# First block's attentions: one group of attention products a step, then the dense products

## Chip, cores and metric
One NeuronCore of a Trainium2 chip runs the whole program. The metric is the device time of one execution in microseconds (us), smaller is better; the kernel before takes 2327.96 (median of 3 runs, 2321.61 to 2328.72).

## What is computed
Two transformer blocks on 256 tokens (and, in the first block, 256 context tokens) of width 1024, all in float32. The first block has two layers. Each layer: a gated feed-forward net, three attentions that share one input projection and one output projection, and a second feed-forward net. The second block (a recurrent mix, latent attention, differential attention, a convolutional feed-forward net) is not touched by the change. The attentions of a layer, cut to what matters:

```python
p = u @ w_in[l]                       # q, k, v of all heads
y_w = _window_attn(q_w, k_w, v_w, ck_w, cv_w, sink_win[l])      # 6 heads, window and sink
y_g = _global_attn(q_g, k_g, v_g, ck_g, cv_g)                   # 4 heads, q and k normed
y_n = _neighbourhood_attn(q_n, k_n, v_n, ck_n, cv_n, rpb_nbr[l])  # 6 heads, bias
h = h + gm * (concatenate([y_w, y_g, y_n]) @ w_out[l])
if not last:                          # layer 0 alone: the context attends to itself
    hc = hc + cgm * (yc @ w_out[l])
```

Each attention is softmax(q k^T / 8 + mask or bias) v over the 256 tokens and the 256 context tokens.

## The kernel before
**Dense products.** Activations lie with features on the partitions and tokens along the free dimension. A float32 product is done as three with rounded halves: `three` (L1212) issues high x high (L1214), high x low (L1215) and low x high (L1216) for one k-step of 128 rows. The weights come from memory in panels of 1024 KB into two buffers (`raw`); ScalarE makes the high half of a panel (`whi`), VectorE the low one (`wlo`). In the stretches of the change this is done in four pieces, `split_piece` (L588): pieces 0 and 2 on ScalarE (L598, L600), 1 and 3 on VectorE (L608).

**Order.** Every engine executes its own instructions strictly in the order in which the program issues them. The engines meet by semaphores only. So the order of the Python calls is the schedule: a call that issues to ScalarE queues there behind all that earlier calls put there.

**The stretch of the change** is a layer's attention stage (`for l in range(L1)`, about L1590 to L2066). Two things are interleaved there by hand.

One is the generator `program` (L1875): the input projection in 18 tiles (`in_tile`, L1663; the order of q, k and v tiles is `IN_TILES`, L61) and the output projection in 16 (`out_tile`, L1818), with small jobs in between or inside a tile: `turn` (L1789) multiplies a q or k chunk by a permutation, for the rotary embedding, whose three VectorE operations are L1800, L1801 and L1803; `v_turn` (L1726) transposes a value tile from `v_feat`. A tile or job takes one of two accumulator banks (6 and 7) by `next_bank` (L1633), which makes TensorE wait until what was last in that bank is copied out. A job inside a tile takes the other bank than that tile, the one that the next tile will take. The copying out (`evacuate`, L1718 for q, L1720 for k, L1712 for v, L1738 for the turned values) is issued at the next `flush` (L1871), in the second k-step of the following tile or near its end. The generator yields a cost in us (0.69 for a k-step of 512 columns, 0.36 for 256); `fill(us)` (L1906) takes from it until the costs are used up. `need` (L1916) takes from it until an input is prepared, and its costs are taken off the following fills.

The other is the attention itself, one unit at a time: a unit is two heads (a chunk c of 128 features), a stream (0 the tokens, 1 the context, in layer 0 alone) and a half of 128 queries. Layer 0 has 32 units, four to a chunk (stream 0 twice, then stream 1 twice; "a quad"); layer 1 has 16, all of stream 0. For a unit:

- `scores` (S, product L1936): queries by keys, 512 keys for stream 0, 256 for stream 1, into a pair of banks (0 and 1 or 2 and 3). It waits for the exponentials of the unit two before.
- `exponentials` (exp): on VectorE mask or bias (L1959), maximum (L1960), for windowed heads the sink (L1964, L1966), for global ones the norm (L1970); on ScalarE two exponentials (L1974) and for windowed heads one more of the sink (L1978).
- `normalise` (norm): VectorE, reciprocal (L1987, with L1986 for the sink) and two scalings of the probabilities (L1990).
- `transposes(i, s)` (T0 and T1, product L2004): four transposes of the probabilities of head s into bank 4, which ScalarE copies out (`probs_t`, L2011). Both begin with a wait of TensorE for norm and for the last copy out of bank 4. For a context unit T1 does both heads, and T0 does nothing but that wait.
- `values` (V, L2026), at each odd unit: 16 products for stream 0, 8 for stream 1, into bank 5.
- `split_y` (y), at each odd unit: y_hi on ScalarE (L2037), y_lo on VectorE (L2039).

Step i of the loop at L2045 issues, before the change, in this order: T0(i-2), S(i+1), exp(i), norm(i-1), a fill of half the step's share, T1(i-2), V(i-3), y(i-4), a fill of the other half. A step's share is 4 us of costs in stream 0 and 2 in stream 1. `share` and what a fill takes in all are as before in the changed kernel.

Of the kernel before, what the change touches and what calls it, by code (L numbers as in the profile page):

```python
# [748 lines left out]
def build(nc, ins, out):  # L749
# [48 lines left out]
    def cst(name, width=P, k=0):  # L798
        o = CC.at[name] + k
        if o >= CC.kept:  # L800
            return tables[0][:, o - tables[1]:o - tables[1] + width]
        return const[:, o:o + width]

    def vcol(name, k=0, width=1):
        o = VC.at[name] + k
        if o >= VC.kept:
            return vec_2[:, o - VC.kept:o - VC.kept + width]
        return vec[:, o:o + width]
# [294 lines left out]
    def root_table(function=ACT.Sqrt):  # L1103

        act.do(act.q.activation(root_warm[:, :], cst("eps", 1), function))
# [451 lines left out]
    for l in range(L1):  # L1557
# [348 lines left out]
        def fill(us):  # L1906

            ahead[0] += us
            while ahead[0] > 0 and not all_heads_left[0]:
                cost = next(work)  # L1910
                if cost is None:
                    all_heads_left[0] = True
                else:
                    ahead[0] -= cost

        def need(*keys):  # L1916

            while any(k not in prepared for k in keys):
                ahead[0] -= next(work)

        units = [(c, stream, qt) for c in ATT for stream in range(streams_q) for qt in range(2)]
# [3 lines left out]
        def kind_of(i):  # L1925
            return head_at(units[i][0], 0)[0]

        def scores(i):
            c, stream, qt = units[i]
            kc = head_at(c, 0)[2]  # L1930
            need(("q", c), ("k", kc))
            o, key0 = stream * S + qt * P, stream * S
            pe.after(prepared["q", c], prepared["k", kc], (st.s_ev, st.groups), marks[i - 2]["exp"] if i >= 2 else None)
            for s in range(2):
                rows_ = slice(64 * s, 64 * s + 64)
                r = pe.q.matmul(banks[2 * (i % 2) + s][:, 0:T - key0], qT[rows_, c, o:o + P], kT[rows_, kc, key0:T],  # L1936
                                start=True, stop=True)
            marks[i]["scores"] = pe.do(r)

        def exponentials(i):  # L1940
            c, stream, qt = units[i]
            kind = kind_of(i)
            nk = T - stream * S
            b = bank_pairs[i % 2][:, :].rearrange("p (s n) -> p s n", s=2)
            k, m = i % 3, marks[i]
            dve.after(m["scores"])
            bias = None
            if stream == 0 and kind == "win":
                bias, left = cst("win_mask", S, qt * S).rearrange("p (o n) -> p o n", o=1).to_broadcast([P, 2, S]), b[:, :, 0:S]
                dve.after(tab_ready)  # L1950
            if stream == 0 and kind == "nbr":
                need(("nbr", c))
                dve.after(prepared["nbr", c])
                first = NBR_DR - NBR_ROWS - 2 * qt
                h0_ = 2 * (c - 5)
                bias = nbr[:, h0_:h0_ + 2, first:first + NBR_ROWS, :].rearrange("p h r c -> p h (r c)")
                left = b[:, :, 0:S]
            if bias is not None:
                dve.after(dve.do(dve.q.tensor_tensor(left, left, bias, ALU.add)))  # L1959
            mx = dve.do(dve.q.tensor_reduce(out=stat[:, k, 0, :], in_=b[:, :, 0:nk], axis=AX.X, op=ALU.max, negate=True))  # L1960
            scale = [1.0, 1.0]
            if kind == "win":
                dve.after(mx, sink_ready)
                mx = dve.do(dve.q.tensor_tensor(stat[:, k, 0, :], stat[:, k, 0, :], neg_sink[:, 2 * c:2 * c + 2], ALU.min))  # L1964
                dve.after(mx)
                over = dve.do(dve.q.tensor_tensor(stat[:, k, 2, :], stat[:, k, 0, :], vcol(("sink", l), 2 * c, 2), ALU.add))  # L1966
            if kind == "glob":
                o = 8 * (c - 3) + 2 * (2 * stream + qt)
                dve.after(mx, prepared["rms"])
                mx = dve.do(dve.q.tensor_tensor(stat[:, k, 0, :], stat[:, k, 0, :], rms[:, o:o + 2], ALU.mult))  # L1970
                scale = [rms[:, o + s:o + s + 1] for s in range(2)]
            act.after(mx, marks[i - 3]["transposed"] if i >= 3 else None)
            for s in range(2):
                m["exp"] = act.do(act.q.activation(pbuf[k][:, s, 0:nk], b[:, s, 0:nk], ACT.Exp, bias=stat[:, k, 0, s:s + 1],  # L1974
                                                   scale=scale[s], accum_out=stat[:, k, 1, s:s + 1]))
            if kind == "win":
                act.after(over)
                m["sink"] = act.do(act.q.activation(stat[:, k, 2, :], stat[:, k, 2, :], ACT.Exp))  # L1978

        def normalise(i):  # L1980
            c, stream, qt = units[i]
            nk = T - stream * S
            k, m = i % 3, marks[i]
            dve.after(m["exp"], m.get("sink"))
            if "sink" in m:
                dve.after(dve.do(dve.q.tensor_tensor(stat[:, k, 1, :], stat[:, k, 1, :], stat[:, k, 2, :], ALU.add)))  # L1986
            dve.after(dve.do(dve.q.reciprocal(stat[:, k, 3, :], stat[:, k, 1, :])))  # L1987
            for s in range(2):
                pb = pbuf[k][:, s, 0:nk]
                m["norm"] = dve.do(dve.q.tensor_scalar(pb, pb, stat[:, k, 3, s:s + 1], None, ALU.mult))  # L1990
# [3 lines left out]
        def transposes(i, s):  # L1994
            c, stream, qt = units[i]
            nt = 4 - 2 * stream
            k, m, quad = i % 3, marks[i], i // 2
            pe.after(m["norm"], copied[0])
            if stream and s == 0:
                return  # L2000
            heads_ = range(2) if stream else [s]
            for x, hd in enumerate(heads_):
                for t in range(nt):
                    r = pe.q.transpose(banks[4][:, (x * nt + t) * P:(x * nt + t + 1) * P], pbuf[k][:, hd, t * P:(t + 1) * P],  # L2004
                                       cst("ident"))
            m["transposed"] = pe.do(r)
            act.after(m["transposed"], quads_done.get(quad - 2))
            dst = ptb[quad % 2][:, s, :, qt * P:(qt + 1) * P] if not stream else ptb[quad % 2][:, :, 0:nt, qt * P:(qt + 1) * P]
            src = banks[4][:, :].rearrange("p (t q) -> p t q", q=P) if not stream else \
                banks[4][:, :].rearrange("p (s t q) -> p s t q", s=2, q=P)  # L2010
            copied[0] = act.do(act.q.activation(dst, src, ACT.Copy))  # L2011
            m["copied"] = copied[0]

        def values(i):

            if i % 2 == 0:
                return
            c, stream, _ = units[i]
            nt, quad = 4 - 2 * stream, i // 2
            kc = head_at(c, 0)[2]  # L2020
            need(("v", kc))
            pe.after(prepared["v", kc], marks[i]["copied"], quads_done.get(quad - 1))
            for t in range(nt):
                for s in range(2):
                    vo = head_at(c, s)[3]
                    r = pe.q.matmul(banks[5][64 * s:64 * s + 64, 0:S], vt[:, t + 2 * stream, vo:vo + HD],  # L2026
                                    ptb[quad % 2][:, s, t, :], start=(t == 0), stop=(t == nt - 1))
            marks[i]["pv"] = pe.do(r)
# [16 lines left out]
        for i in range(len(units) + 4):  # L2045
            here = min(i, len(units) - 1)
            share = 1.33 if units[here][1] == 0 else 0.67
            if 2 <= i < len(units) + 2:
                transposes(i - 2, 0)
            if i + 1 < len(units):  # L2050
                scores(i + 1)
            if i < len(units):
                exponentials(i)
            if 1 <= i <= len(units):
                normalise(i - 1)
            fill(1.5 * share)
            if 2 <= i < len(units) + 2:
                transposes(i - 2, 1)
            if 3 <= i < len(units) + 3:
                values(i - 3)  # L2060
            if i >= 4:
                split_y(i - 4)
            fill(1.5 * share)
            if i == len(units):
                root_table()
        for _ in work:  # L2066
# [1125 lines left out]
```

## Time and profile before

| | us |
|---|---|
| median of 3 runs | 2327.96 (2321.61 to 2328.72) |
| profiled execution | 2326.03 |
| its span in the trace | 2324.7 |
| TensorE busy | 2260.5 (97%) |
| VectorE busy | 1490.9 (64%) |
| ScalarE busy | 964.4 (41%) |
| attention stage of layer 0, in the span | about 430 to 640 |
| attention stage of layer 1 | about 1400 to 1550 |

How to read it: the span runs from the first to the last recorded instruction of one execution. PE is TensorE's products, PEld its weight loads, DVE is VectorE, ACT is ScalarE, POOL is GpSimd. TensorE's products are pipelined, so the time of one is best read from the start of one to the start of the next, and "busy" is no measure of how well it is used. A float32 product with full precision appears as more than one record. In a wait, the engine and line behind the arrow are what released it. PEclk is the clock that TensorE was granted, as a share of 2.4 GHz.

### The profile page before, as it was taken

How to read it: one execution, taken by the hardware profiler on the slowest of the kernel's cores; microseconds unless marked ns; L12 is line 12 of the kernel's file. 1: busy time of each engine (PE TensorE's matmuls, PEld its weight loads, DVE VectorE, ACT ScalarE, POOL GpSimd, SP SyncE). 2: the span in 40 equal slices, each digit the busy share in tenths (PEclk: the TensorE clock that was granted, in tenths of full speed). 3: DMA queues.
4: the chain of work that ended last, by engine and by line, in shares of the span. 5: the costliest groups of instructions: out<-in, count | busy, mean ns of one | idle time of the engine just before them, and what ended most of it. 6: DMA issues, size and time to landing. Idle time of an engine off the chain costs nothing. (4 is left out here: it accounts for less than half of the span.)

```text
span 2324.7 us, 37251 instructions
## 1 busy us (share of the span) xinstructions
PE 2260.5 (97%) x14432; PEld 1920.7 (83%) x14432; DVE 1490.9 (64%) x2302; ACT 964.4 (41%) x1555; POOL 393.9 (17%) x381
## 2 busy tenths in 40 slices
PE   9999999999999999999999999989999999999998
PEld 6888887666778888888888876679998998898998
DVE  5756766465676666676564345666667766777874
ACT  5222224455442222242222244554446335656763
POOL 1000001100010000000000011049996575000000
PEclk9999999999999999999999999999999999999999
DMA  7654543311234444434443323124554332244544
GB/s 297 221 187 162 180 162 129 106 37 55 73 118 181 171 173 161 170 139 163 162 180 130 100 103 108 58 89 178 178 175 157 110 103 91 77 157 159 189 165 143
DMA packets 53911, 331.05 MB, mean 142 GB/s; under 512 B 6688, under 2 KB 7968, under 8 KB 23328
## 3 DMA queue, kind: packets, MB, share of 16 engines
q1 hardware_dynamic: 50336, 319.15, 38.6%
q0 software_dynamic: 3456, 10.25, 1.6%
q8 instruction: 83, 1.36, 0.2%
q14 instruction: 36, 0.29, 0.0%
HBM read 325.56 MB, written 3.80 MB: 142 GB/s over the span
## 5 line engine op out<-in xcount | busy, mean ns | idle before, releaser
L1214 PE MATMUL bank<-u_hi,whi 128*128 128x512 f32 (+1 forms) x2352 | 805.2, 342 | 4.8 <-ACT qT L1716 1.6
L1215 PE MATMUL bank<-u_lo,whi 128*128 128x512 f32 (+1 forms) x2352 | 789.7, 336 | 0.0
L1216 PE MATMUL bank<-u_hi,wlo 128*128 128x512 f32 (+1 forms) x2352 | 789.6, 336 | 0.0
L585 DVE TENSOR_TENSOR wlo<-raw,whi 128x2048 fp32r<-128x2048 f32 (+2 forms) x203 | 423.6, 2086 | 307.5 <-ACT whi L581 297.8
L1214 PEld LDWEIGHTS bank<-u_hi,whi 128*128 128x128 f32 x2352 | 443.1, 188 | 82.3 <-issue 27.8
L581 ACT ACTIVATE whi<-raw 128x2048 fp32r<-128x2048 f32 (+2 forms) x203 | 345.5, 1702 | 346.3 <-PE bank L1216 296.0
L1216 PEld LDWEIGHTS bank<-u_hi,wlo 128*128 128x128 f32 x2352 | 443.3, 188 | 47.5
L1215 PEld LDWEIGHTS bank<-u_lo,whi 128*128 128x128 f32 x2352 | 442.9, 188 | 44.6 <-issue 0.2
L1289 ACT ACTIVATE sil<-bank 128x512 f32<-128x512 f32 (+1 forms) x88 | 48.0, 545 | 519.4 <-PE bank L1216 516.6
L1214 PE MATMUL bank<-hidden_hi,whi 128*128 128x512 f32 x528 | 205.4, 389 | 0.0
L1215 PE MATMUL bank<-hidden_lo,whi 128*128 128x512 f32 x528 | 205.4, 389 | 0.0
L1216 PE MATMUL bank<-hidden_hi,wlo 128*128 128x512 f32 x528 | 205.4, 389 | 0.0
L643 POOL TENSOR_TENSOR wlo<-raw,whi 128x512 fp32r<-128x512 f32 x16 | 21.4, 1335 | 971.6 <-ACT whi L627 971.5
L943 DVE SCALAR_TENSOR_TENSOR bank<-raw,c_row 128x1024 f32<-128x1024 f32 x128 | 157.2, 1228 | 8.5 <-DMA raw<-in_stream 7.4
L1407 POOL TENSOR_TENSOR rel_bias_map<-rel_bias_map,bucket_step 128x384 f32<-128x384 f32 x124 | 158.1, 1275 | 10.4
L943 DVE SCALAR_TENSOR_TENSOR raw<-raw,bank 128x1024 f32<-128x1024 f32 x128 | 155.7, 1217 | 0.0
L1293 DVE TENSOR_TENSOR prod<-sil,bank 128x512 f32<-128x512 f32 (+1 forms) x88 | 54.6, 621 | 157.3 <-ACT sil L1289 154.3
L608 DVE TENSOR_TENSOR wlo<-raw,whi 128x1024 fp32r<-128x1024 f32 (+2 forms) x84 | 99.3, 1193 | 73.3 <-ACT whi L598 69.7
L1404 POOL TENSOR_SCALAR bucket_step<-in_bucket,bucket_steps 128x384 f32<-128x384 f32 x124 | 131.5, 1060 | 12.4
L1216 PEld LDWEIGHTS bank<-hidden_hi,wlo 128*128 128x128 f32 x528 | 99.1, 188 | 20.7
L1215 PEld LDWEIGHTS bank<-hidden_lo,whi 128*128 128x128 f32 x528 | 99.1, 188 | 20.6
L1214 PEld LDWEIGHTS bank<-hidden_hi,whi 128*128 128x128 f32 x528 | 99.1, 188 | 20.4
(450 smaller groups left out, 3204.9 us busy)
## 6 DMA issues: line engine op xcount, KB each, us to landing
raw<-in_stream SPq DMA_DIRECT2D x229, 1024.0 KB, 4.8
raw<-in_stream SPq DMA_DIRECT2D x80, 704.0 KB, 4.0
first_ada<-in_stream SPq DMA_DIRECT2D x8, 1024.0 KB, 16.7
raw<-in_stream SPq DMA_DIRECT2D x8, 768.0 KB, 4.2
skew<-rpb_rows POOLq DMA_DIRECT2D x8, 336.0 KB, 6.3
nbr_bias<-skew POOLq DMA_DIRECT2D x24, 112.0 KB, 5.9
h<-in_tokens SPq DMA_DIRECT2D x4, 512.0 KB, 5.6
raw<-in_stream SPq DMA_DIRECT2D x8, 256.0 KB, 16.8
```

Of the source, the lines that this page charges most:

```text
L581: a.activation(self.hi[to][:, 0:n], raw[:, 0:n], ACT.Copy).then_inc(self.s_hi, 1)
L585: v.tensor_tensor(self.lo[to][:, 0:n], raw[:, 0:n], self.hi[to][:, 0:n].bitcast(F32), ALU.subtract).then_inc(self.s_lo, 1)
L608: r = v.q.tensor_tensor(self.lo[to][:, cols], self.raw[slot][:, cols], self.hi[to][:, cols].bitcast(F32), ALU.subtract)
L643: r = v.q.tensor_tensor(self.lo[to][:, cols], self.raw[slot][:, cols], self.hi[to][:, cols].bitcast(F32), ALU.subtract)
L943: r = dve.q.scalar_tensor_tensor(out=product, in0=w, scalar=1.0, in1=rows, op0=ALU.mult, op1=ALU.mult, accum_out=to)
L1214: pe.q.matmul(dst, w[0], x[0], start=start, stop=False)
L1215: pe.q.matmul(dst, w[0], x[1], start=False, stop=False)
L1216: return pe.q.matmul(dst, w[1], x[0], start=False, stop=stop)
L1289: act.q.activation(sil[par][:, 0:n], banks[2 * par][:, 0:n], ACT.Silu).then_inc(s_sil, 1)
L1293: dve.q.tensor_tensor(prod[par][:, 0:n], sil[par][:, 0:n], banks[2 * par + 1][:, 0:n], ALU.mult).then_inc(st.s_ev, 1)
L1404: z = pool.do(pool.q.tensor_scalar(step[:, :], bucket[:, :], 1.0 - start, steps[:, hh, b + 1:b + 2], ALU.add, ALU.mult))
L1407: z = pool.do(pool.q.tensor_tensor(rel[:, hh, :], rel[:, hh, :], step[:, :], ALU.add))
```

## The change
In each step the second half's transposes T1 of unit i-2, the scores, the values and y now stand together at the step's start; norm(i-1) is issued ahead of them, exp(i) behind them; T0, now of unit i-1, closes the group; then comes one fill with the costs of both. Everything else is the same.

```diff
@@ -2045,22 +2045,21 @@
         for i in range(len(units) + 4):
             here = min(i, len(units) - 1)
             share = 1.33 if units[here][1] == 0 else 0.67
+            if 1 <= i <= len(units):
+                normalise(i - 1)
             if 2 <= i < len(units) + 2:
-                transposes(i - 2, 0)
+                transposes(i - 2, 1)
             if i + 1 < len(units):
                 scores(i + 1)
-            if i < len(units):
-                exponentials(i)
-            if 1 <= i <= len(units):
-                normalise(i - 1)
-            fill(1.5 * share)
-            if 2 <= i < len(units) + 2:
-                transposes(i - 2, 1)
             if 3 <= i < len(units) + 3:
                 values(i - 3)
             if i >= 4:
                 split_y(i - 4)
-            fill(1.5 * share)
+            if i < len(units):
+                exponentials(i)
+            if 1 <= i < len(units) + 1:
+                transposes(i - 1, 0)
+            fill(3 * share)
             if i == len(units):
                 root_table()
         for _ in work:
```

Step i in the changed kernel: norm(i-1), T1(i-2), S(i+1), V(i-3), y(i-4), exp(i), T0(i-1), fill.

## Rows read from the trace of the kernel before

**Rows 1.** The page's first line: the span.
```profile
span 2324.7 us, 37251 instructions
```

**Rows 2.** Windows: length; busy PE, PEld, DVE, ACT, POOL; PEclk, DMA share, GB/s.
```profile
430.00:640.00 210.00, 202.82 (x1056) 140.96 (x1056) 128.21 (x284) 108.37 (x253) 0.00 (x0) 1.00 0.15 55
1400.00:1550.00 150.00, 140.87 (x855) 105.36 (x855) 91.05 (x171) 77.03 (x159) 8.01 (x12) 1.00 0.24 78
```

**Rows 3.** Waits of TensorE, 430 to 640: us in total, times, longest.
```profile
PE bank L1936 <- ACT probs_t L2011: 1.6, 2, 0.8
...
PE bank L1795 <- ACT qT L1718: 0.9, 2, 0.7
...
PE bank L1936 <- DVE probs L1990: 0.8, 1, 0.8
```

**Rows 4.** Waits of TensorE, 1400 to 1560.
```profile
PE bank L1732 <- ACT inv_norm_diagonal L1712: 3.3, 2, 1.9
PE bank L2004 <- ACT probs_t L2011: 2.0, 2, 1.2
```

**Rows 5.** Timeline, TensorE, steps 7 and 8 of layer 0: start, duration, instruction, [idle before].
```profile
474.92 0.60 PE L2004 MATMUL bank<-const,probs 128*128 128x128 f32 x4
476.30 1.13 PE L1936 MATMUL bank<-kT,qT 64*128 64x512 f32 x4 [0.78 <-ACT probs_t L2011]
```

**Rows 6.** Timeline, TensorE, block edges in layer 0.
```profile
485.59 0.70 PE L1936 MATMUL bank<-kT,qT 64*128 64x256 f32 x4
486.22 0.50 PE L1214 MATMUL bank<-u_hi,whi 128*128 128x512 f32 x1
486.56 0.39 PE L1215 MATMUL bank<-u_lo,whi 128*128 128x512 f32 x1
486.79 0.39 PE L1216 MATMUL bank<-u_hi,wlo 128*128 128x512 f32 x1
...
487.72 0.60 PE L2004 MATMUL bank<-const,probs 128*128 128x128 f32 x4
488.07 0.48 PE L1214 MATMUL bank<-u_hi,whi 128*128 128x512 f32 x1
```

**Rows 7.** Timeline of three engines, steps 11 and 12 of layer 0.
```profile
499.19 0.60 ACT L2011 ACTIVATE probs_t<-bank 128x512 f32<-128x512 f32 x1 [1.48 <-PE bank L2004]
...
499.68 0.38 ACT L2037 ACTIVATE y_hi<-bank 128x256 fp32r<-128x256 f32 x1
...
500.09 0.42 DVE L2039 TENSOR_TENSOR y_lo_k<-bank,y_hi 128x256 fp32r<-128x256 f32 x1 [2.94 <-ACT y_hi L2037]
...
502.61 0.69 ACT L1974 ACTIVATE probs<-bank,stat 128x512 f32<-128x512 f32 x1 [2.06 <-DVE stat L1964]
...
503.47 0.60 PE L2004 MATMUL bank<-const,probs 128*128 128x128 f32 x4
503.61 0.69 DVE L1959 TENSOR_TENSOR bank<-bank,tables 128x512 f32<-128x512 f32 x1
...
504.00 1.95 PE L2026 MATMUL bank<-probs_t,v 128*64 128x256 f32 x16
504.10 0.60 ACT L2011 ACTIVATE probs_t<-bank 128x512 f32<-128x512 f32 x1
...
507.23 0.59 ACT L1738 ACTIVATE v<-bank 128x512 f32<-128x512 f32 x1
```

**Rows 8.** Groups by line and form, 430 to 640: busy us, mean ns, idle before.
```profile
L608 DVE TENSOR_TENSOR wlo<-raw,whi 128x1024 fp32r<-128x1024 f32 x20 | 24.4, 1220 | 11.0 <-ACT whi L598 10.8 <-ACT whi L600 0.2
...
L1990 DVE TENSOR_SCALAR probs<-probs,stat 128x512 f32<-128x512 f32 x32 | 14.1, 484 | 0.6
...
L2039 DVE TENSOR_TENSOR y_lo_k<-bank,y_hi 128x256 fp32r<-128x256 f32 x10 | 4.3, 425 | 30.5 <-ACT y_hi L2037 30.5
```

**Rows 9.** Windows behind layer 1's attentions, columns as in rows 2.
```profile
1555.00:1560.00 5.00, 3.11 (x22) 2.54 (x21) 4.22 (x9) 2.31 (x6) 4.55 (x6) 1.00 0.62 210
1560.00:1570.00 10.00, 8.22 (x31) 7.11 (x32) 8.50 (x11) 6.89 (x14) 9.08 (x11) 0.51 0.00 0
```

## The prediction

> **What bounds the kernel now.** I read the page's head first, then the table of windows, the waits of TensorE, then the timeline of three engines over a few steps. The span is 2324.7 us [rows 1]; the profiled execution took 2326.03, so 1.33 lie around the span, and the median of the three runs, 2327.96, is 1.93 above it. The sum below is made against 2326.03. The two stretches that the change touches are the attentions of layer 0 and of layer 1 [rows 2]: TensorE is busy for 202.8 of 210 and 140.9 of 150 us at a granted clock of 1.00, VectorE and ScalarE for only 50 to 60%. So TensorE's work and its waits set the time here, and all that the change can win is some of the 16 us that are not busy, or the gaps hidden in busy time; what it can lose is a new wait of TensorE on the two engines behind it.
>
> The named waits are few: in layer 0 three of 0.8 us ahead of a score product (two put down to the copy of the transposes, one to the scaling) and 0.7 of a turn job [rows 3]; in layer 1 two jobs that turn a value tile, 1.9 and 1.4, and two transposes behind a copy, 1.2 and 0.8 [rows 4]. One of the three is seen at 474.92: T1 starts, its fill turned out empty, the next step's T0 call (no transposes for a context unit, only its wait) wants the copy, and S starts 1.38 us after T1, where 0.53 would do [rows 5].
>
> **What is moved.** No instruction is added or removed, no DMA either; SP's and POOL's orders stay. Only the order on TensorE, VectorE and ScalarE changes.
>
> *Block edges.* A change of product costs about 0.1 us: after S (485.59 to 486.22, 0.63) the first dense product takes 0.34 to the next, 0.23 being the usual [rows 6]. T ahead of dense takes 0.35 to the next start, and ahead of V 0.53 [rows 6, 7]. So grouping mostly passes the 0.1 on to the neighbour: S now has T0 or V behind it in place of dense. No row shows S ahead of V. Bounds: nothing saved, or 0.2 for each of the 24 steps with V, 4.8. I take 1.0 in layer 0 and 1.6 in layer 1. TensorE: Matmul & The Clock Gate of the Trainium skill (Part 2, LDWEIGHTS step) says that the next weights are loaded while the present product runs; by that an edge is free, grouping saves nothing and the sum would come out at 2342.7 instead of 2340.1. The 0.34 beside 0.23 speaks for a small price, so the row is taken.
>
> *Waits removed.* T1 and the next T0 call no longer touch across an empty fill of 2 us: 3 times 0.8 in layer 0. Going through the generator with the planner's costs, the turn job of q1 is reached later behind its evacuation, 0.15 in place of 0.7. Together 2.9.
>
> *The chain that is now one piece.* In a step with y (odd i), ScalarE's order becomes: copy of T1, y_hi, exp(i), copy of T0, and only then what the fill issues; VectorE's: norm, y_lo, mask, max, and then the fill's. Before, exp(i) stood ahead of T1 and of y, in the half before, and could run ahead of TensorE: the mask of 503.61 is that of step 13 and began before TensorE had started V of step 12, so the evacuation of turned values, issued behind exp(13), came at 507.23, in time [rows 7]. Now mask waits for y_lo, that for y_hi, that for the copy of T1, that for T1. The rows of one such passage give the times from the start of T1 [rows 7]: copy +0.63 (503.47 to 504.10), y_hi +1.12 (499.19 to 499.68 on top), y_lo +1.53, then mask and max, first exp +4.05 (3.42 after the copy), both exps and the sink's over at +5.54 (502.61 to 504.10 is 1.49), copy of T0 +6.1, an evacuation of the fill +6.7. VectorE is free for the fill at about +4.2. TensorE enters the fill much earlier: T1 0.53, S of a context unit 0.63, then T0 wants the copy of T1, which is there at 1.38, then 0.35: +1.73. Six dense products take 1.50 (486.22 to 487.72) [rows 6].
>
> A job inside a tile takes the bank that the next tile will want, so the next tile waits for the job's evacuation. With the planner's costs (0.69 us a k-step of 512 columns, 0.36 of 256) I listed what each fill issues; the places in layer 0 where an evacuation stands in an odd step of token units:
> - step 13: tile 12 wants its bank at 1.73+1.50 = 3.23, turned v2 is out at 6.7: 3.5.
> - step 9: tile 10 at 3.23, the first rope product of q1 at 4.2+0.4 (a 128x256 operation like y_lo, 0.42): 1.4.
> - step 5: the same for k0, a unit without mask (0.73 less): 0.7.
> - step 25: out tile 1 at 1.73+3.0, turned v4 at 6.35 (no sink): 1.7.
> Sum 7.3.
>
> *T0's own waits, layer 0.* T1's copy is not there when S is a short one: 1.38-1.16 = 0.22, in 7 quads (a quad: the four units of a chunk), 1.5. And norm(i-1), 1.05 with its reciprocal (two of 0.48 [rows 8]), now stands behind the previous fill's split pieces (1.22 each on VectorE [rows 8]) with only T1, S and V to hide it. That falls on one step in four; by hand it comes to 0 to 1.5 a quad with T1 behind the late copy of T0 in it; I take 0.5, 8 times: 4.0.
>
> Layer 0: 7.3+1.5+4.0-2.9-1.0 = +8.9.
>
> *Layer 1* (token units only, each T0 real). Step 7: the value tile's evacuation is out at 6.7; TensorE wants it at 0.53+1.13+0.40, six dense 1.50, then four narrow k-steps 1.44 = 5.0: 1.7. Step 15: 6.35 against 1.38+0.35+1.50 = 3.2, so 3.1, in place of 1.4: +1.7. Step 12: 2.5 in place of 1.9, +0.6. Where `need` has already used up the fill (steps 5 and 13), T0 and T1 of one unit touch and T1 waits for a copy that is behind exp: +0.4 each over the waits of today. Step 9, where norm is behind four pieces and a rope: 1.2. Two smaller ones (steps 4 and 8): 0.8. Together 6.8, less 1.6 for edges: +5.2.
>
> Sum: 2326.03+8.9+5.2 = **2340.1**, against the median 2327.96 +0.5%. What this measurement tells from no change is 0.3%, 7 us: 2321 to 2335 is the same.
>
> **Rivals.**
> (a) *Run-ahead is kept.* If exp(i) is not held, since ScalarE had been idle for 1.48 us when its copy came [rows 7] and need not be as late as I think, none of the new waits comes, the old ones go: 2.9, 1.2+0.8 of layer 1, and 4.8 of edges: 2326.03-9.7 = 2316. It decides where the fill's first evacuation is out before +3.2. Against it: VectorE sits idle 30.5 us ahead of y_lo for y_hi [rows 8], so y holds the queue already. 0.10.
> (b) *The waits absorb each other.* After one long wait the two engines have caught up, and the next waits shrink; the T0 terms (1.5, 4.0, 1.2) vanish and a third of the 7.3 and 6.8: 2340.1-6.7-4.7 = 2329. The gaps of one quad that I laid out by hand came partly to this. 0.27.
> (c) *The clock falls in the new waits.* After TensorE's pauses of 1555 to 1560 (3.11 busy of 5) the granted clock is 0.51 for the ten us that follow, which is the 1.2 GHz level [rows 9]; such a fall costs about half of its 10 us, 5. If steps 12 to 13 of layer 0 and 15 of layer 1 do that too: 2350. TensorE: Matmul & The Clock Gate (Part 1) says that an idle array is put at 1.2 GHz and a busy one gets 2.4; by that rule my waits could do it. For it: my longest wait, 3.5, is longer than any named one here. Against: 1.9 left the clock at 1.00 [rows 2, 4]. 0.10.
> My forecast keeps 0.53. That the dense work does not follow in one run is true where `need` issues it between T1 and S (layer 1, steps 3, 5, 13), and is in the sum.
>
> **Numbers.** Faster: (a), 0.10. Same: (b), 0.27. Slower: forecast and (c), 0.63. Range: from 2325, under (b), to 2351, over (c), leaving out (a) and the tails of both.
>
> **What would show it.** Right: named waits of dense products for the turned values (L1738) and the rope (L1800) of 1 to 4 us in layer 0; the mask of an odd step always behind y_lo; TensorE's waits in layer 0 up from 4 to some 12 us; no S waiting 0.78 behind a copy; the rest of the kernel as before. Wrong: if TensorE's named waits stay under 8 us over both layers, my chain is not the mechanism; if they are there and the time is still 2328, edges were worth far more than 0.1.

## The result, and the profile of the changed kernel

The changed kernel took 2346.74 us (median of 4 runs, 2344.23 to 2347.75), the one before 2325.88 (4 runs): ratio 1.0092, 95% interval 1.0077 to 1.0108, so 20.9 us slower, which is more than the 0.3% that this measurement can tell. The profiled execution took 2344.23, with a span of 2342.9.

The head of the profile, the changed kernel (span; busy time, share and instructions of each engine), and its group of dense products (busy, mean ns, idle before):
```profile
span 2342.9 us, 37247 instructions
...
PE 2258.3 (96%) x14432; PEld 1918.1 (82%) x14432; DVE 1494.9 (64%) x2302; ACT 964.4 (41%) x1555; POOL 393.3 (17%) x381
...
L1214 PE MATMUL bank<-u_hi,whi 128*128 128x512 f32 (+1 forms) x2352 | 802.8, 341 | 11.3 <-ACT v L1738 5.0
```
The work is the same; what grew is TensorE's idle time. The idle time ahead of the dense products of L1214 went from 4.8 to 11.3 us, and 5.0 of it are waits for turned values; before, the largest single part was 1.6, behind a copy of q (L1716).

TensorE's waits in the changed kernel, 425 to 650 (layer 0), which answer to [rows 3]: us in total, times, longest.
```profile
PE bank L1214 <- ACT v L1738: 4.8, 2, 3.2
PE bank L2004 <- DVE probs L1990: 4.3, 5, 1.6
PE bank L1214 <- DVE prod L1800: 1.5, 2, 1.2
```
The same view, 1400 to 1580 (layer 1), which answers to [rows 4]:
```profile
PE bank L1732 <- ACT inv_norm_diagonal L1712: 6.6, 3, 3.0
PE bank L2004 <- ACT probs_t L2011: 5.0, 3, 2.2
PE bank L1214 <- ACT v L1738: 1.8, 1, 1.8
PE bank L2004 <- DVE probs L1990: 1.0, 1, 1.0
```
Windows of the changed kernel, columns as in [rows 2]: both stretches, then the ten us around the longest wait of layer 0 (3.23, which ends at 514.57), and three windows of layer 1, around waits that end at 1520.65 (2.11 us), 1535.48 (2.25) and 1550.15 (2.96).
```profile
430.00:640.00 210.00, 191.90 (x1001) 131.68 (x1002) 120.82 (x270) 102.94 (x246) 0.00 (x0) 0.99 0.14 50
1400.00:1560.00 160.00, 141.04 (x819) 104.10 (x818) 89.51 (x167) 80.13 (x166) 12.96 (x19) 0.98 0.25 81
...
510.00:520.00 10.00, 6.76 (x26) 4.98 (x24) 6.53 (x14) 3.95 (x9) 0.00 (x0) 0.83 0.00 0
...
1520.00:1530.00 10.00, 9.35 (x44) 8.12 (x45) 3.19 (x4) 4.07 (x7) 0.00 (x0) 0.83 0.24 81
1530.00:1540.00 10.00, 7.75 (x36) 3.90 (x36) 5.66 (x10) 4.86 (x12) 0.00 (x0) 0.83 0.25 100
...
1550.00:1560.00 10.00, 9.71 (x81) 8.66 (x82) 4.68 (x8) 5.16 (x8) 0.00 (x0) 1.00 0.30 97
```
TensorE is busy for 191.9 of 210 us where it was 202.8, and three windows within the stages have a granted clock of 0.83; in the kernel before the stages' windows all have 1.00.

To compare whole stages I measure each from its key-norm product (L1778) to the first statistics product (L1062) behind it. Layer 0 took 209.3 us before and 221.7 after (+12.4), layer 1 148.9 and 159.3 (+10.4). TensorE's named waits in these stretches add up to 6.9 and 9.2 before, 16.6 and 17.7 after.

The predicted chain is in the timeline of three engines, step 13 of layer 0, changed kernel (start, duration, engine, line and operation, [idle before]); it answers to [rows 7]:
```profile
507.95 0.60 PE L2004 MATMUL bank<-const,probs 128*128 128x128 f32 x4
...
508.48 0.70 PE L1936 MATMUL bank<-kT,qT 64*128 64x256 f32 x4
508.58 0.60 ACT L2011 ACTIVATE probs_t<-bank 128x512 f32<-128x512 f32 x1 [3.12 <-PE bank L2004]
509.08 0.38 ACT L2037 ACTIVATE y_hi<-bank 128x256 fp32r<-128x256 f32 x1
...
509.32 0.63 PE L2004 MATMUL bank<-const,probs 128*128 128x128 f32 x4
509.49 0.42 DVE L2039 TENSOR_TENSOR y_lo<-bank,y_hi 128x256 fp32r<-128x256 f32 x1 [2.65 <-ACT y_hi L2037]
...
509.83 0.69 DVE L1959 TENSOR_TENSOR bank<-bank,tables 128x512 f32<-128x512 f32 x1
...
512.01 0.69 ACT L1974 ACTIVATE probs<-bank,stat 128x512 f32<-128x512 f32 x1 [2.55 <-DVE stat L1964]
...
513.92 0.60 ACT L1738 ACTIVATE v<-bank 128x512 f32<-128x512 f32 x1
...
514.57 0.59 PE L1214 MATMUL bank<-u_hi,whi 128*128 128x512 f32 x1 [3.23 <-ACT v L1738]
```
From T1's start: y_hi at +1.13, y_lo +1.54, first exp +4.06, turned values begun +5.97 and out at +6.57. The prediction had +1.12, +1.53, +4.05 and +6.7. T0 starts at +1.37, where it would have started at +1.16 without the copy: that is the hidden 0.22, and it carries no name in the waits.

### The profile page after: what moved, and what is told of

The parts are those of the page before. It is cut to its first block and busy times, and to the rows that moved or that the text cites. A ratio compares the mean times of both kernels' runs of the same rounds, so it can differ in the third digit from the quotient of the medians.

```text
span 2342.9 us, 37247 instructions
## 1 busy us (share of the span) xinstructions
PE 2258.3 (96%) x14432; PEld 1918.1 (82%) x14432; DVE 1494.9 (64%) x2302; ACT 964.4 (41%) x1555; POOL 393.3 (17%) x381
## 5 line engine op out<-in xcount | busy, mean ns | idle before, releaser
L1214 PE MATMUL bank<-u_hi,whi 128*128 128x512 f32 (+1 forms) x2352 | 802.8, 341 | 11.3 <-ACT v L1738 5.0
L1214 PEld LDWEIGHTS bank<-u_hi,whi 128*128 128x128 f32 x2352 | 443.3, 188 | 72.1 <-issue 8.1
L1214 PE MATMUL bank<-hidden_hi,whi 128*128 128x512 f32 x528 | 205.4, 389 | 0.0
L1404 POOL TENSOR_SCALAR bucket_step<-in_bucket,bucket_steps 128x384 f32<-128x384 f32 x124 | 131.4, 1060 | 12.4
L1214 PEld LDWEIGHTS bank<-hidden_hi,whi 128*128 128x128 f32 x528 | 99.1, 188 | 20.6
```

The costliest lines, as they stand in the source:

```text
L1214: pe.q.matmul(dst, w[0], x[0], start=start, stop=False)
L1404: z = pool.do(pool.q.tensor_scalar(step[:, :], bucket[:, :], 1.0 - start, steps[:, hh, b + 1:b + 2], ALU.add, ALU.mult))
```

## Experiments

All ratios are to the kernel before, timed on the same chip in the same batch. The edits are shown against the changed kernel where nothing else is said. "Stages" are the lengths of layer 0 and layer 1, measured as above.

### First batch: which placement makes the loss

**Exponentials ahead of T1.** Only exp(i) moves, to right behind the scaling.
```diff
                 normalise(i - 1)
+            if i < len(units):
+                exponentials(i)
             if 2 <= i < len(units) + 2:
                 transposes(i - 2, 1)
...
                 split_y(i - 4)
-            if i < len(units):
-                exponentials(i)
```


> The changed kernel with exp(i) put ahead of T1, S, V and y (order of a step: norm, exp, T1, S, V, y, T0, fill). Theory (the chain T1, copy, y_hi, y_lo, mask, max, exp stands in one piece ahead of all that the fill issues on ScalarE and VectorE): the waits for turned values, rope and evacuations (about 5 us in layer 0, 6 in layer 1, and 3 to 5 of clock lost behind them) go, T0's waits for norm stay at about 5 us: 2329 to 2335. Rival, the position of T0 right behind norm is what costs: no more than 2 us better than the changed kernel, 2343 to 2348. Rival, one long fill as such: the same, 2343 to 2348.

Measured: 2364.48 us, 1.0165 (1.0148 to 1.0182), stages 228.3 and 166.1. TensorE's waits in this kernel, 425 to 650:
```profile
PE bank L2004 <- ACT probs_t L2011: 9.3, 7, 3.5
PE bank L1214 <- ACT probs_t L2011: 8.4, 10, 1.7
```
No theory of mine had this. exp(i) is now ahead of T1's copy on ScalarE, and T0 at the step's end wants that copy. "exp early" is good only while no copy that TensorE needs in the same step is behind it. The waits for the turned values did go, as my theory said; they were replaced by a dearer one.

**T0 late.** The step begins with T0(i-2) and has T1(i-2) ahead of the fill; exp stays behind y.
```diff
-                transposes(i - 2, 1)
+                transposes(i - 2, 0)
...
-            if 1 <= i < len(units) + 1:
-                transposes(i - 1, 0)
+            if 2 <= i < len(units) + 2:
+                transposes(i - 2, 1)
```


> The changed kernel with T0 and T1 of the same unit i-2, T0 at the group's start and T1 at its end (norm, T0, S, V, y, exp, T1, fill): T0 has a whole step more for norm, the chain stays. Theory of the chain: only T0's waits for norm (5.3 us named) go, and the short wait for the copy: 2337 to 2343. Rival, T0 behind norm is the cost: 2325 to 2331. Rival, the single fill: 2343 to 2348.

Measured: 2337.01 us, 1.0036 (1.0023 to 1.0049), stages 207.0 and 158.9. The time lies in the range that I gave, but not for the reason: layer 0 came back whole and layer 1 not at all. The timeline of the three engines around step 13 of layer 0, this kernel:
```profile
501.91 0.38 ACT L2037 ACTIVATE y_hi<-bank 128x256 fp32r<-128x256 f32 x1
...
502.81 0.42 DVE L2039 TENSOR_TENSOR y_lo<-bank,y_hi 128x256 fp32r<-128x256 f32 x1
...
503.14 0.69 DVE L1959 TENSOR_TENSOR bank<-bank,tables 128x512 f32<-128x512 f32 x1
...
504.53 0.70 PE L1936 MATMUL bank<-kT,qT 64*128 64x256 f32 x4
```
In layer 0 the units alternate, and in an odd token step T0(i-2) belongs to a context unit and does nothing. So y_hi waits for no copy of this step, and y and exp of step 13 run at 501.9 to 503.1, before TensorE reaches the step's first product at 504.53. In layer 1 every T0 is real and its copy stands ahead of y_hi as T1's does in the changed kernel; there the waits are as long:
```profile
PE bank L1732 <- ACT inv_norm_diagonal L1712: 6.6, 3, 3.0
PE bank L2004 <- ACT probs_t L2011: 6.2, 5, 2.3
```
So what counts is whether y_hi, and with it y_lo and exp, hangs on a transpose of the same step. Part of layer 1's loss here is the clock: from 1529 to 1536, around the end of the wait of 3.0, it stands at 0.52, close to the 1.2 GHz level; by this I estimate some 3 us.

**One fill, old placement.** Order T0, S, exp, norm, T1, V, y as before, but both fills in one at the end.
```diff
-            if 1 <= i <= len(units):
-                normalise(i - 1)
             if 2 <= i < len(units) + 2:
-                transposes(i - 2, 1)
+                transposes(i - 2, 0)
             if i + 1 < len(units):
                 scores(i + 1)
+            if i < len(units):
+                exponentials(i)
+            if 1 <= i <= len(units):
+                normalise(i - 1)
+            if 2 <= i < len(units) + 2:
+                transposes(i - 2, 1)
...
                 split_y(i - 4)
-            if i < len(units):
-                exponentials(i)
-            if 1 <= i < len(units) + 1:
-                transposes(i - 1, 0)
             fill(3 * share)
```


> The kernel before, with nothing but its first half fill moved behind y (T0, S, exp, norm, T1, V, y, one fill): products grouped and one fill, but exp ahead of T1 and y, and T0 a step behind norm. Theory of the chain: no long wait for evacuations; T1 now follows T0 by S alone and waits for T0's copy only where S is short; 2324 to 2332. Rival, the single long fill costs by itself: 2338 to 2346. If block edges are worth what was taken (2.6) and nothing else moves: 2323.

Measured: 2322.78 us, 0.9979 (0.9969 to 0.9988), stages 207.9 and 148.3, a little under the 2324 to 2332 of my theory and nowhere near the rival's 2338. That the dense products follow in one run costs nothing; the loss is made by where exp and T0 stand.

**Exponentials held in the old order.** Two fills as before, T0 early, but exp(i) and norm(i-1) behind y.
```diff
-            if 1 <= i <= len(units):
-                normalise(i - 1)
             if 2 <= i < len(units) + 2:
-                transposes(i - 2, 1)
+                transposes(i - 2, 0)
             if i + 1 < len(units):
                 scores(i + 1)
+            fill(1.5 * share)
+            if 2 <= i < len(units) + 2:
+                transposes(i - 2, 1)
...
                 exponentials(i)
-            if 1 <= i < len(units) + 1:
-                transposes(i - 1, 0)
-            fill(3 * share)
+            if 1 <= i <= len(units):
+                normalise(i - 1)
+            fill(1.5 * share)
```


> The kernel before, with nothing but exp and norm moved behind T1, V and y (T0, S, half fill, T1, V, y, exp, norm, half fill): two fills, nothing grouped, but exp is held by y as in the changed kernel. Theory of the chain: evacuations issued in the second fill come late as in the changed kernel, those of the first don't: 2331 to 2340. Rivals (single fill, T0 behind norm): neither is there, 2324 to 2329.

Measured: 2404.55 us, 1.0325 (1.0304 to 1.0347), stages 261.2 and 179.3, mean granted clock 0.976 against 0.989. The sign is as expected, the size is far off, and it is not a clean test: I had moved the scaling behind exp too, so T0 of the next step waits for it. TensorE's waits, 425 to 650:
```profile
PE bank L2004 <- DVE probs L1990: 12.4, 6, 3.1
PE bank L1936 <- ACT stat L1978: 5.9, 3, 2.0
PE bank L1936 <- ACT probs L1974: 4.9, 2, 3.2
```
It shows only how dear the two engines' lateness can get; it doesn't tell how much of it is exp's hold. The second batch does that with one swap.

### Second batch: the swap alone, and the edges

**Exponentials ahead of y.** The changed kernel with exp(i) and y exchanged.
```diff
-            if i >= 4:
-                split_y(i - 4)
             if i < len(units):
                 exponentials(i)
+            if i >= 4:
+                split_y(i - 4)
```


> The changed kernel with exp(i) and y(i-4) exchanged (norm, T1, S, V, exp, y, T0, fill): VectorE's statistics need no longer wait for T1, its copy, y_hi and y_lo, while T0 stays right behind norm and the fill stays one. Theory (two costs, each of its own: exp held by y, worth about 10 us in layer 1 and 6 to 8 in layer 0 with the clock; T0 a step too early for norm, 4 to 5 in layer 0 alone): stage of layer 1 from 159.3 back to 149 to 152 us, of layer 0 from 221.7 to 213 to 216, in all 2327 to 2334. Rival, layer 0's loss is all T0's position: layer 0 stays at 219 to 222, in all 2336 to 2341.

Measured: 2329.13 us, 1.0015 (1.0005 to 1.0025), stages 209.7 and 152.9. TensorE's waits, 425 to 650, then 1400 to 1560:
```profile
PE bank L1214 <- ACT v L1738: 1.2, 1, 1.2
PE bank L2004 <- DVE probs L1990: 0.9, 2, 0.6
...
PE bank L2004 <- ACT probs_t L2011: 4.0, 3, 2.5
PE bank L1732 <- ACT inv_norm_diagonal L1712: 2.2, 2, 1.1
```
One exchange gives back 17.6 of the 20.9 us. Layer 0 came back further than the 213 to 216 that I expected: I had given T0's position a cost of 4 to 5 us of its own there, and 209.7 against 209.3 before leaves little room for it. It also cuts T0's waits for the scaling from 4.3 to 0.9, though T0 and the scaling have not moved: those waits came from the same lateness.

**One fill, and the context unit's T0 call returns at once.** This edit and the next are shown against "One fill, old placement". The call does nothing for a context unit but wait; here it returns before the wait.
```diff
+            if stream and s == 0:
+                return
             pe.after(m["norm"], copied[0])
-            if stream and s == 0:
-                return
```


> one_fill with T0's call for a context unit made to return ahead of its wait (it issues no work). In one_fill no wait of layer 0 is left that comes from it, so both theories expect one_fill's time, 2320 to 2325; if the wait also holds back weight loads at the edges, up to 2 us less.

Measured: 2324.02 us, 0.9993 (0.9983 to 1.0003), stages 207.9 and 148.3. No gain over one fill alone (0.9979): the intervals overlap, and the stages are the same to 0.1 us.

**One fill with the pending split pieces issued ahead of exp.**
```diff
                 scores(i + 1)
+            flush()
             if i < len(units):
                 exponentials(i)
```


> one_fill with the finished tile's evacuation issued ahead of exp instead of behind it (flush before exponentials). If order on ScalarE is what sets the waits, the remaining ones of dense products and jobs for evacuations (rope 1.1, jobs 0.7 and 0.7, turned values 0.6) shrink: 1 to 3 us under one_fill, 2318 to 2324. If exp is delayed by it and that counts, slower than one_fill by 1 to 3.

Measured: 2321.81 us, 0.9982 (0.9971 to 0.9993), stages 206.8 and 147.8: 1.1 and 0.5 shorter than with one fill, and not to be told from it by the time.

**The kernel before, with the early return.** Same edit of the T0 call in the kernel before, nothing else.

> The kernel before with the same early return for a context unit's T0. By the waits named before (three of 0.8 in layer 0), 2.4 us less than before: 2322 to 2326. If those 0.8 only move to the next wait: the same as before, 2325 to 2329.

Measured: 2324.52 us, 0.9998 (0.9988 to 1.0008), stages 207.7 and 150.6. Layer 0 is 1.6 us shorter and layer 1 1.7 longer, though layer 1 has no context units and runs the same order as before, and TensorE's named waits there are the same 9.2. The difference is the clock: behind the value job's wait of 1.88, which is in the trace of the kernel before too and left the clock at 1.00 there, this execution fell. This kernel's trace:
```profile
1498.33 0.66 PE L1732 MATMUL bank<-const,inv_norm_diagonal 128*128 128x128 f32 x4 [1.88 <-ACT inv_norm_diagonal L1712]
...
1499.57 3.36 PE L2026 MATMUL bank<-probs_t,v 128*64 128x256 f32 x16
```
The values take 3.36 in place of 1.95, and the windows 1490 to 1500 and 1500 to 1510 have a granted clock of 0.95 and 0.88. So the stage of layer 0 shows a gain of 1.6 us for the three waits of 0.78 [rows 3, 5], but the time of the kernel can't confirm it.

### Third batch: which link of the chain, and the best order

**y_lo alone behind exp.** `split_y` is parted: y_hi stays ahead of exp on ScalarE, y_lo goes behind exp on VectorE.
```diff
-            hi = act.do(act.q.activation(y_hi[:, c, col], banks[5][:, 0:S], ACT.Copy))
-            dve.after(hi)
+            marks[i]["y_hi"] = act.do(act.q.activation(y_hi[:, c, col], banks[5][:, 0:S], ACT.Copy))
+
+        def split_y_low(i):
+
+            if i % 2 == 0:
+                return
+            c, stream, _ = units[i]
+            col = slice(stream * S, stream * S + S)
+            dve.after(marks[i]["y_hi"])
...
                 exponentials(i)
+            if i >= 4:
+                split_y_low(i - 4)
```


> The changed kernel with y parted: y_hi stays ahead of exp on ScalarE, y_lo goes behind it on VectorE (norm, T1, S, V, y_hi, exp, y_lo, T0, fill). If the link that holds exp is VectorE waiting for y_hi, this alone frees it, though ScalarE still has copy and y_hi in front: like exp_mid, 2326 to 2332, stages near 210 and 153. Rival, ScalarE's order (copy of T1 and y_hi ahead of exp) holds it: 2338 to 2347.

Measured: 2321.19 us, 0.998 (0.9967 to 0.9992), stages 205.3 and 148.5. The timeline of the three engines around step 13 of layer 0:
```profile
503.31 0.69 DVE L1959 TENSOR_TENSOR bank<-bank,tables 128x512 f32<-128x512 f32 x1
...
505.61 0.60 PE L2004 MATMUL bank<-const,probs 128*128 128x128 f32 x4
...
507.00 0.69 ACT L1974 ACTIVATE probs<-bank,stat 128x512 f32<-128x512 f32 x1
...
507.15 0.42 DVE L2046 TENSOR_TENSOR y_lo<-bank,y_hi 128x256 fp32r<-128x256 f32 x1 [1.50 <-ACT y_hi L2037]
...
508.90 0.63 ACT L1738 ACTIVATE v<-bank 128x512 f32<-128x512 f32 x1
...
509.57 0.50 PE L1214 MATMUL bank<-u_hi,whi 128*128 128x512 f32 x1 [0.57 <-ACT v L1738]
```
The mask now runs 2.30 us ahead of T1 instead of 1.88 behind it, the turned values begin at +3.29 instead of +5.97, and the dense product waits 0.57 instead of 3.23. The first exp still stands behind the copy and y_hi on ScalarE, yet it starts at +1.39 in place of +4.06, so ScalarE's order is not what held it. One instruction of 0.42 us on an engine that is 64% busy carried the whole loss: VectorE stood in y_lo waiting for y_hi, and mask and max stood behind it. The time is under the 2326 to 2332 that I expected, and 8 us better than with the whole of y behind exp: both stages are 4.4 us shorter, of which named waits make up 2.7 in layer 0 and 2.1 in layer 1 and one fall of the clock in layer 1 about 1.7. That is one execution of each; why y_hi is better ahead of exp was not tried further.

**T0 late with exp ahead of y.** Against the changed kernel both edits, of "T0 late" and of "Exponentials ahead of y".

> t0_late with exp and y exchanged (norm, T0, S, V, exp, y, T1, fill); beside exp_mid only T0's position differs, and exp is held in neither. Theory (T0's position costs only while exp is held): layer 0 within 2 us of exp_mid's 209.7, layer 1 within 3 of 152.9; 2324 to 2330. Rival, T0 right behind norm has a price of its own: 4 us or more under exp_mid, 2325 or less, with layer 0 at 205 or less.

Measured: 2324.18 us, 0.999 (0.9977 to 1.0003), stages 206.9 and 149.1. Layer 1, which T0 late alone had left at 158.9, is cured by the exchange; layer 0 had nothing left to cure (207.0). Both stages are a little better than with exp ahead of y alone, by 2.8 and 3.8 us, more than the 2 and 3 that my theory allowed and less than the rival asked of layer 0 (205 or less). T0's position may have a small price of its own; this run does not settle it.

**The best order found.** T0, S and V first, the pending pieces, then exp and norm, then T1 and y, then one fill.
```diff
-            if 1 <= i <= len(units):
-                normalise(i - 1)
             if 2 <= i < len(units) + 2:
-                transposes(i - 2, 1)
+                transposes(i - 2, 0)
...
                 values(i - 3)
-            if i >= 4:
-                split_y(i - 4)
+            flush()
             if i < len(units):
                 exponentials(i)
-            if 1 <= i < len(units) + 1:
-                transposes(i - 1, 0)
+            if 1 <= i <= len(units):
+                normalise(i - 1)
+            if 2 <= i < len(units) + 2:
+                transposes(i - 2, 1)
+            if i >= 4:
+                split_y(i - 4)
```


> one_fill_flush with V between S and T1 in place of behind T1 (T0, S, V, flush, exp, norm, T1, y, one fill). In layer 1 five waits of T1 for T0's copy are left, 4.5 us; V lies between in every second step, so one to three of them go: 1 to 3 us under one_fill_flush, 2318 to 2322. If the two waits at empty fills are the large ones, nothing: 2321 to 2323.

Measured: 2316.53 us (2312.82 to 2318.02), 0.9957 (0.994 to 0.9973), stages 203.8 and 145.1. It beats both kernels, the one before by 0.43%, and is better than the 2318 to 2322 that I expected. TensorE's waits, 1400 to 1560:
```profile
PE bank L2004 <- ACT probs_t L2011: 3.3, 4, 1.2
...
PE bank L1732 <- ACT inv_norm_diagonal L1712: 0.7, 1, 0.7
```
The turn jobs' waits for a value tile, 3.3 before and 6.6 in the changed kernel, are down to 0.7.

## Why the prediction was right, and where its sizes were off

The sign, the range and the mechanism held. Forecast were 14.1 us more than the profiled execution of before; measured are 18.2 by the profiled executions and 20.9 by the medians. Within the two stages it was 22.8, since outside them the profiled execution of the changed kernel was 4.6 us quicker (last section).

| term, us | predicted | measured |
|---|---|---|
| layer 0, steps 13, 9, 5, 25 | 3.5, 1.4, 0.7, 1.7 | 3.23, 1.22, 0.30, 1.57 |
| layer 0, T0 behind a short S | 1.5 | 1.7 |
| layer 0, all named waits, more than before | 8.4 | 9.7 |
| layer 1, steps 7, 15, 12 | 1.7, 3.1, 2.5 | 1.76, 2.96, 2.11 |
| layer 1, all named waits, more than before | 6.8 | 8.5 |
| block edges, layers 0 and 1 | -1.0, -1.6 | -2.7, about -1.5 |
| lower clock | 0 | about 5 |

**The chain: shown.** The moment at which each part of step 13 happens was right to 0.02 us up to the first exp. That VectorE's wait in y_lo is the link is shown by two kernels: the exchange of exp and y, and y_lo alone put behind exp.

**Rival (a), run-ahead kept: refuted.** Its argument for itself was ScalarE's idle 1.48 us. The idle time was real and useless: the engine was held by order, not by load. What (a) describes is what the kernel does when y_lo is out of the way: 2321.19, not 2316.

**Rival (b), the waits absorb each other: refuted for the size of the sum.** T0's waits for the scaling (4.0 forecast) did come, 4.3. That the size met is in part luck: I had put 0.5 on each of eight quads, and what came were five waits of 0.2 to 1.6. But the rival had a point: those waits shrink to 0.9 when the chain is cut, so they were a result of the chain and not a second cause.

**Rival (c), the clock: true in part, and the step that was mis-sized.** I kept the clock at 1.00 in the forecast and priced its fall only in the rival. Three windows of ten us stand at 0.83. What it costs shows in TensorE's own times: the dense run of step 13 was 5.12 us longer than its products need, of which 3.23 is the wait, so some 1.9 is the clock. The timeline of TensorE in layer 1, changed kernel, behind the wait at an empty fill:
```profile
1535.48 1.11 PE L2004 MATMUL bank<-const,probs 128*128 128x128 f32 x4 [2.25 <-ACT probs_t L2011]
1536.53 2.08 PE L1936 MATMUL bank<-kT,qT 64*128 64x512 f32 x4
```
S goes on for 2.08 where it took 1.13 before [rows 5], which is the 1.2 GHz level. 17% of each of three windows is 1.7, 5.1 in all. My argument against it was that a wait of 1.9 had left the clock at 1.00. That was the reading of one execution, and it does not hold: the same wait of 1.88 was followed by a fall in the run of the kernel before with the early return. Nor does the length of a wait decide it. In the changed kernel the falls came behind waits of 3.23, 2.11 and 2.25, and none behind the 2.96 that ends at 1550.15. The Trainium skill, TensorE: Matmul & The Clock Gate, Part 1, says that an idle array is put at 1.2 GHz; the falls behind waits agree, the window behind the 2.96 shows that a wait alone does not bring one. In the kernels with the chain cut less clock is lost: with exp ahead of y two windows of layer 1 are at 0.87 and 0.96, one fall behind a wait of 2.54; with y_lo alone behind exp none falls inside the stages. But "T0 late with exp ahead of y" has one fall in layer 0 (600 to 610 at 0.83), behind waits of 1.57 and 0.69. What decides it between one wait and the next these traces do not show.

**T1 behind T0's copy at empty fills: mis-sized.** I put the two places of layer 1 at 0.4 each over today's waits. Measured, the three waits for the copy came to 5.0 against 2.0 before: 3.0 more, not 0.8. The rows of VectorE and ScalarE around T0 say why, changed kernel, layer 1:
```profile
1531.17 0.43 DVE L2039 TENSOR_TENSOR y_lo_k<-bank,y_hi 128x256 fp32r<-128x256 f32 x1 [2.24 <-ACT y_hi L2037]
1531.51 0.69 DVE L1959 TENSOR_TENSOR bank<-bank,nbr_bias 128x512 f32<-128x512 f32 x1
...
1532.58 0.66 PE L2004 MATMUL bank<-const,probs 128*128 128x128 f32 x4
1533.49 0.69 ACT L1974 ACTIVATE probs<-bank,stat 128x512 f32<-128x512 f32 x1 [2.36 <-DVE stat L1960]
...
1534.84 0.59 ACT L2011 ACTIVATE probs_t<-bank 128x512 f32<-128x512 f32 x1
```
The products are done by about 1533.2; the copy begins 1.6 us later, behind both exps. I had reckoned that exp would be nearly over when T0 ends. It isn't, since the mask of this step, too, starts only behind y_lo.

**Edges: right in kind, forecast too small in layer 0.** I counted them through TensorE's timeline of layer 0. The first dense product behind S or V takes 0.34 to the next in both kernels, against 0.23; there are 38 such places before and 17 after, 21 × 0.11 = 2.3 saved. The last dense product ahead of S takes 0.33; 11 places before, 1 after: 1.0 saved. Behind T the first dense product takes 0.32, 15 places and 18: 0.3 lost; the rest of T's neighbours comes to 0.3 lost too. Net 2.7. S itself takes 0.63 (256 columns) or 1.06 (512) whatever stands behind it, and V 1.01 or 1.88. In layer 1 the saving is a difference and no count, so it takes in whatever else changed there: the stage less its named waits and less 3.4 for the clock went from 139.7 to 138.2. By the rule that I weighed (the Trainium skill, the same page, Part 2, LDWEIGHTS step: the next weights load while the present product runs) edges would be free; the trace disagrees by 0.1 us an edge. This is what grouping gains, some 4 us over both layers, and the change handed it back several times over.

**One fill alone** shows the same from the other side: it has few block edges as well, but V now stands behind T1 and T1 behind T0 with only S between, and by the same count it comes to +0.3; its stage less named waits is 202.5 against 202.4 before. Its gain of 1.4 in layer 0 is shorter waits.

**Which of my signs were seen.** Waits of dense products for L1738 and L1800 of 1 to 4 us in layer 0: three of four (the fourth 0.30). The mask of an odd step behind y_lo: yes. TensorE's waits in layer 0 from 4 to some 12: they were 6.9 over the whole stage before and went to 16.6. No S behind a copy for 0.78: yes.

**What stays open.** The terms of the table leave about 2 us of the 22.8 unplaced; some of it lies in pauses too short for a named wait, such as a last dense product ahead of T that takes up to 0.50 in place of 0.23. These pauses are not added up here. I didn't try y_lo parted from y_hi within the best order, nor whether it could shed the 5.6 and 7.0 us of waits that are left there.

## What to carry to other kernels

When pieces of work are put together for the sake of one engine, look at the order that the two engines behind it get, and ask of each instruction which can wait: what is queued behind it that had been running ahead? A short instruction that waits for another engine (here y_lo, 0.42 us) belongs behind whatever doesn't depend on it; an engine that is half idle can still be late. And when new waits of 2 us or more are forecast for TensorE, put the lower clock behind them into the range: in these traces it fell behind some waits of about 2 to 3 us and not behind others, and each fall cost about 1.7 us or more.

## What the runs showed that I had not expected

**Dense products of one shape ran at two spacings at a granted clock of 1.00.** The windows of TensorE in the second block's dense stretch, the kernel before:
```profile
2180.00:2190.00 10.00, 10.00 (x87) 10.00 (x87) 8.00 (x14) 6.89 (x11) 0.00 (x0) 1.00 0.47 157
```
and the changed kernel, which reaches the same place 23 us later:
```profile
2203.00:2213.00 10.00, 10.00 (x90) 10.00 (x90) 8.21 (x15) 7.79 (x14) 0.00 (x0) 1.00 0.61 210
```
Both are busy throughout and wait for nothing, with products of 128x256. One takes 279 ns with 0.118 to the next, the other 276 with 0.113. Over this stretch of about 110 us that is worth some 4 us, and the changed kernel's offset in fact falls there from 24 to 18.6. Nothing in the change touches this code, and the traces of all the other runs, with their various orders, show 0.118 there. What sets the spacing no view shows; the runs of one kernel differ by as much (2321.61 to 2328.72 before). So a term of under 5 us can't be read from the end of the span, and I read stages instead.

**An exchange of two calls, for engines that are 41% and 64% busy, was worth 17.6 us**, more than all of the edges (2.7), the T0 call's waits (1.6 in a stage, no measurable gain in the time) and the flush (1.1 and 0.5 in the stages) together.
